# Weights laid out in DRAM as the stream of tiles, and the opening's modulation tiles as stationary operands, in an f32 transformer kernel on one Trainium2 core

## The reference

```python
shift, scale, gate = jnp.split(jax.nn.silu(c) @ w_mod + b_mod, 3, axis=-1)
shift_c, scale_c, gate_c = jnp.split(jax.nn.silu(c_ctx) @ w_mod + b_mod, 3, axis=-1)
hx = rmsnorm(x, g_pre) * (1 + scale[:, None]) + shift[:, None]
hc = rmsnorm(ctx, g_pre) * (1 + scale_c) + shift_c
q, k, v, ga, uf, gf, zc, bc, cc, gc = split_cols(hx @ w_in, PROJ_SIZES)
```

## Time and profile before

| | |
|---|---|
| Median of 3 runs | 1942.44 us (1939.84 to 1943.55) |
| The profiled execution: its time | 1941.8 us |
| Its span in the profile | 1940.0 us |
| Granted TensorE clock, mean | 0.995 |
| VectorE, ScalarE, GpSimd busy | 43%, 42%, 36% of the span |
| Read from DRAM | 178.10 MB |
| DMA packets | 199589, of which 168957 are under 2 KB |

### The profile page before, as it was taken

One profiled execution on the slowest core, in us unless ns is written; L12 is line 12 of the kernel. 1 busy time (PEld: TensorE's weight loads), 2 busy tenths in 40 slices (PEclk: granted clock), 3 DMA queues, 4 the chain that ended last, 5 costly groups with the idle time before them and its releaser, 6 DMA issues.

```text
span 1940.0 us, 26619 instructions
## 1 busy us (share of the span) xinstructions
PE 1895.1 (98%) x10294; PEld 1610.3 (83%) x10294; DVE 827.5 (43%) x1871; ACT 818.7 (42%) x1573; POOL 693.5 (36%) x542
## 2 busy tenths in 40 slices
PE   8999989999899999999999999999999999999997
PEld 4897889878689888888988888888888898888886
DVE  3657866265567264576511110037267551111003
ACT  3321268363238465685332222126477432323222
POOL 0522502125430344212455454544420344544442
PEclk9999999999999999999999999999999999999999
DMA  9536322113230224211243433223320233332321
GB/s 283 166 109 217 106 45 55 44 44 116 80 87 34 90 88 118 85 34 55 77 109 87 109 87 130 87 79 109 110 82 23 69 84 109 87 106 90 130 87 44
DMA packets 199589, 181.95 MB, mean 94 GB/s; under 512 B 34823, under 2 KB 168957, under 8 KB 199465
## 3 DMA queue, kind: packets, MB, share of 16 engines
q1 hardware_dynamic: 193432, 168.93, 29.0%
q10 hardware_dynamic: 6032, 11.33, 1.9%
HBM read 178.10 MB, written 5.41 MB: 95 GB/s over the span
## 4 chain that ended last, share of the span: by engine, by line
PE 84%; DVE 5%; ACT 3%; issue 2%; POOL 2%; DMA 2%; SPq 0%; ACTq 0%; DVEq 0%
PE ps L1368 23%; PE ps L1370 22%; PE ps L1369 22%; PE ps L1962 3%; PE ps L1459 3%; PE ps L1879 3%; POOL w_lo L760 2%; DMA raw<-in_w_in 2%; PE ps L1426 2%; PE ps L1445 2%; PE ps L1980 2%; DVE acc L2172 1%; PE ps L1489 1%; ACT w_hi L815 1%; PE ps L1389 1%
## 5 line engine op out<-in xcount | busy, mean ns | idle before, releaser
L760 POOL TENSOR_TENSOR w_lo<-raw,w_hi 128x512 fp32r<-128x512 f32 (+2 forms) x507 | 668.5, 1351 | 1147.7 <-ACT w_hi L815 1147.6
L815 ACT ACTIVATE w_hi<-raw 128x1024 fp32r<-128x1024 f32 (+3 forms) x256 | 252.4, 1032 | 300.9 <-PE ps L1370 190.9
L1368 PE MATMUL ps<-g_hi,w_lo 128*128 128x512 f32 (+1 forms) x928 | 348.4, 375 | 1.4 <-POOL w_lo L760 1.4
L1369 PE MATMUL ps<-g_lo,w_hi 128*128 128x512 f32 (+1 forms) x928 | 347.5, 374 | 0.0
L1370 PE MATMUL ps<-g_hi,w_hi 128*128 128x512 f32 (+1 forms) x928 | 347.4, 374 | 0.0
L1368 PEld LDWEIGHTS ps<-g_hi,w_lo 128*128 128x128 f32 x928 | 174.7, 188 | 33.6 <-issue 1.7
L1370 PEld LDWEIGHTS ps<-g_hi,w_hi 128*128 128x128 f32 x928 | 174.7, 188 | 31.4
L1369 PEld LDWEIGHTS ps<-g_lo,w_hi 128*128 128x128 f32 x928 | 174.7, 188 | 30.8
L1368 PE MATMUL ps<-h_hi,w_lo 128*128 128x512 f32 (+1 forms) x496 | 181.8, 367 | 8.1 <-ACT cz L972 4.5
L2715 DVE TENSOR_TENSOR tmp_f<-ps,tmp_f 128x512 f32<-128x512 f32 x44 | 30.4, 692 | 370.7 <-PE ps L1370 370.7
L1369 PE MATMUL ps<-h_lo,w_hi 128*128 128x512 f32 (+1 forms) x496 | 175.7, 354 | 0.0
(11 more groups left out here) (310 smaller groups left out, 3426.8 us busy)
## 6 DMA issues: line engine op xcount, KB each, us to landing
raw<-in_w_in SPq DMA_DIRECT2D x30, 1024.0 KB, 5.4
raw<-in_w_mod SPq DMA_DIRECT2D x24, 1024.0 KB, 6.1
raw<-in_w_gate SPq DMA_DIRECT2D x44, 512.0 KB, 4.0
raw<-in_w_up SPq DMA_DIRECT2D x44, 512.0 KB, 5.3
raw<-in_w_down SPq DMA_DIRECT2D x22, 1024.0 KB, 4.9
raw<-in_w_out SPq DMA_DIRECT2D x8, 1024.0 KB, 11.6
strips<-bias_rows ACTq DMA_DIRECT2D x18, 256.0 KB, 3.1
raw<-in_w_in SPq DMA_DIRECT2D x16, 256.0 KB, 4.6
```

What stands on the lines that cost most here:

```text
L760: pool.tensor_tensor(w_lo[:, i % SPLIT, a:e], raw_of(what)[:, a:e], w_hi[:, i % SPLIT, a:e].bitcast(F32), ALU.subtract).then_inc(s_tile_lo ...
L815: act.activation(w_hi[:, i % SPLIT, a:b], raw_of(what)[:, a:b], ACT.Copy).then_inc(s_tile_hi.sem, s_tile_hi.nth((what, n)))
L1368: pe.matmul(o, lhs[1], rhs[0], start=first, stop=False)
L1369: pe.matmul(o, lhs[0], rhs[1], start=False, stop=False)
```

## The change

1. The host lays all tiles of the stream one behind another in one array `tiles` (tile, partition, 2048 columns), so that every tile is one transfer with one run of up to 8 KB for each partition. The vectors come as one array `columns` (128 x 118), already turned, loaded by ScalarE's queue into `vec_t`.
2. The opening's modulation tiles become the stationary operand: for each tile 2 x 8 products with a 128 x 128 block of `raw` stationary and `cond` (2 columns) moving, which give columns at once. `mod_row`, `fold`, `first_row`, `first_turn` and both transposes of the vectors are gone.
3. Two of the eight tiles (j = 5 and j = 2) get homes of their own, in the second slots of `w_hi` and `w_lo`, which nothing else uses yet; they are loaded between and behind the halves of `x`. The first query tile is fetched ahead of the last two modulation tiles.
4. The orders of the opening on ScalarE, TensorE, VectorE and GpSimd are rewritten. There are 18 warming products in one piece where there were 7 and 4.

The core of the diff:

```diff
+def _stream():
+
+    s = []
+    for l in range(DEPTH):
+        tiles = _mix_tiles(l)
+        if l == 0:
+            first = [((0, "mod", j), [_rows("w_mod", 0, 0, 256 * j, KD, 256)]) for _, _, j in FIRST]
+            tiles = first[0:3] + [first[5], tiles[0]] + first[6:] + tiles[1:]
+            tiles_apart = first[3:5]
...
+def _laid_out(w):
+
+    stream, apart = _stream()
+    t = np.zeros((len(stream + apart), P, TILE), np.float32)
+    for n, (_, parts) in enumerate(stream + apart):
+        for name, l, row, col, k, c, to, pitch in parts:
+            for j in range(k):
+                t[n, :, to + pitch * j:to + pitch * j + c] = w[name][l, row + P * j:row + P * j + P, col:col + c]
+    return t
...
+        opening = [at(f"opening{i}", [P, TILE], names[where][0] + 4 * TILE) for i, where in enumerate(("w_hi", "w_lo"))]
...
-                for into, src in loads:
-                    sp.dma_start(into(raw[:, n % RAW, :]), src).then_inc(landed_sems[n % RAW], 16)
-                if n < 2:
-                    for dst, src in vectors[4 + 5 * n:9 + 5 * n]:
-                        sp.dma_start(dst, src).then_inc(s_vectors.sem, 16)
-                if n in (2, 3):
-                    t = 2 * (n - 2)
-                    sp.dma_start(res[:, t:t + 2, :], I["x"][0, t * P:(t + 2) * P, :].rearrange("(t p) d -> p t d", p=P)).then_inc(s_x_landed[n - 2].sem, 16)
-                if n == 4:
+                sp.dma_start(raw[:, n % RAW, 0:width(what)], I["tiles"][n, :, 0:width(what)]).then_inc(landed_sems[n % RAW], 16)
+                if n == 2:
+                    for i in range(2):
+                        sp.dma_start(res[:, 2 * i:2 * i + 2, :], I["x"][0, 2 * i * P:(2 * i + 2) * P, :].rearrange("(t p) d -> p t d", p=P)).then_inc(s_x_landed[i].sem, 16)
+                        sp.dma_start(opening[i][:], I["tiles"][len(stream) + i]).then_inc(s_opening[i].sem, 16)
+                if n == 3:
                     sp.dma_start(res_c[:], I["ctx"][0].rearrange("(t p) d -> p t d", p=P)).then_inc(s_x_landed[2].sem, 16)
...
-            for m in range(3):
-                for k in (2 * m, 2 * m + 1):
-                    ctx_lo(0, k)
-                if m > 0:
-                    tile_lo_part(0, 2 * m - 2)
-                    tile_lo_part(0, 2 * m - 1)
-            ctx_lo(0, 6)
-            ctx_lo(0, 7)
+            for p in range(4):
+                tile_lo_part(0, p)
+            for k in range(KD):
+                ctx_lo(0, k)
...
                         if i >= SPLIT:
                             act.wait_ge(s_mm.sem, s_mm.at(("tile", splits[i - SPLIT])))
+                        elif i == 1:
+                            act.wait_ge(s_mm.sem, s_mm.at(("tile", apart[1])))
...
+            act.dma_start(vec_t[:, 0:NV], I["columns"]).then_inc(s_vectors.sem, 16)
+            act.dma_start(ident[:], I["ident"]).then_inc(s_ident.sem, 16)
+            act.wait_ge(s_vectors.sem, 16)
             act.activation(cond[:], vec_t[:, 0:16].rearrange("p (s k) -> p k s", s=2), ACT.Silu).then_inc(s_cond.sem, s_cond.nth(0))
...
             squares(0, 2)
-            first_row(3)
             root((0, "pre", "x"), 8, XT)
+            first_rows(0)
             act.wait_ge(s_x_landed[2].sem, 16)
             squares(0, 4)
             root((0, "pre", "ctx"), 8 + XT, CT)
-            first_row(4)
-            first_rows(0)
-            first_row(5)
+            split_next()
+            first_rows(1)
             first_ctx(0, 0)
-            first_rows(1)
-            first_row(6)
-            split_next()
+            first_rows(2)
             first_ctx(0, 1)
-            first_rows(2)
-            first_row(7)
             first_ctx(0, 2)
             first_rows(3)
...
-            warm(7)
-            pe.wait_ge(s_cond_in.sem, 16 * len(cond_vectors))
-            pe.transpose(ps[:, 7, 0:16], vec[0:16, :], ident[0:16, 0:16]).then_inc(s_vec_mm.sem, s_vec_mm.nth(0))
-            emptied[7] = s_vec_t.after(0)
-            warm(4)
+            warm(18)
...
-                for k in range(KD):
-                    m = pe.matmul(o, cond[:, k, :], raw_of(what)[:, 256 * k:256 * k + 256], start=k == 0, stop=k == KD - 1)
+                for c in range(2):
+                    for k in range(KD):
+                        a = 256 * k + P * c
+                        m = pe.matmul(ps[:, ROW_BANK[i], 2 * c:2 * c + 2], raw_of(what)[:, a:a + P], cond[:, k, :], start=k == 0, stop=k == KD - 1)
...
             first_mod(0)
-            pe.wait_ge(s_vectors.sem, 16 * len(vectors))
-            pe.transpose(ps[:, 2, 0:NV], vec[0:NV, :], ident[0:NV, 0:NV]).then_inc(s_vec_mm.sem, s_vec_mm.nth(1))
-            emptied[2] = s_vec_t.after(1)
-            first_mod(1)
-            first_turn(0)
-            first_mod(2)
-            first_turn(1)
-            first_turn(2)
-            first_mod(3)
-            first_turn(3)
-            first_mod(4)
+            pe.wait_ge(s_ident.sem, 16)
+            for i in range(1, 5):
+                first_mod(i)
             turn_x(0, 0)
             turn_x(0, 1)
-            first_turn(4)
             first_mod(5)
             turn_x(0, 2)
             turn_x(0, 3)
-            turn_ctx(0, 0)
-            first_turn(5)
             first_mod(6)
             turn_x(0, 4)
             turn_x(0, 5)
+            turn_ctx(0, 0)
+            first_mod(7)
             turn_ctx(0, 1)
-            first_turn(6)
-            first_mod(7)
-            turn_ctx(0, 2)
-            first_turn(7)
             q0_rows(0, 0)
             turn_x(0, 6)
             turn_x(0, 7)
+            turn_ctx(0, 2)
             q0_rows(0, 1)
             turn_ctx(0, 3)
...
             for t in range(XT):
                 first_norm(t)
+            first_shift(0)
+            first_in(4)
             first_square(5, 2)
             first_var("ctx", XT, CT, (4,))
-            first_shift(0)
+            first_rows(0)
+            first_in(5)
+            first_shift(1)
             inverse((0, "pre", "ctx"), 8 + XT, CT)
             for t in range(XT, NT):
                 first_norm(t)
-            first_in(4)
-            first_rows(0)
-            first_shift(1)
-            first_in(5)
             first_rows(1)
```

More of the change, by code:

```diff
@@ new lines, in _width, with _rows, _square, _mix_tiles @@
+def _width(what):
+    if what[1] == "up":
+        return 2 * C_HEADS * (QC + HD)
+    if what[1] == "dft":
+        return 4 * (EVEN + ODD) + (4 * EVEN if what[0] < DEPTH - 1 else 0)
+    return {"c": 4 * 416, "av": 4 * 384}.get(what[1], TILE)
+def _rows(name, l, row, col, k, n, to=0, pitch=None):
+    return name, l, row, col, k, n, to, pitch or n
+def _square(name, l, ch, kh):
+    return _rows(name, l, 512 * kh, 512 * ch, 4, 512)
+def _mix_tiles(l):
+    t = []
+    for j in range(2):
+        heads = (2 * j, 2 * j + 4, 2 * j + 1, 2 * j + 5)
+        t.append(((l, "q", j), [_rows("w_in", l, 0, HD * h, KD, HD, HD * i, 256) for i, h in enumerate(heads)]))
+    for what, a in (("kv", 512), ("uf", 1280), ("gf", 1536), ("zc", 1792), ("bc", 2048), ("cc", 2304), ("gc", 2560)):
+        t.append(((l, what), [_rows("w_in", l, 0, a, KD, 256)]))
+    for j in range(2):
+        t.append(((l, "ga", j), [_rows("w_in", l, 0, 768 + 256 * j, KD, 256)]))
+    t.append(((l, "dft"), [_rows("dft", 0, 0, 0, 1, _width((l, "dft")))]))
+    return t
@@ new lines, in _stream @@
+def _stream():
[6 more added lines that the diff above has]
+            tiles_apart = first[3:5]
+        for tile in tiles:
+            s += [(WEIGHED[m], [_square("w_mod", WEIGHED[m][0], *WEIGHED[m][2:])]) for m in GOES_BEFORE.get(tile[0], ())]
+            s.append(tile)
+        s += [((l, "out", ch, kh), [_square("w_out", l, ch, kh)]) for ch, kh in ((0, 1), (0, 0), (1, 0), (1, 1))]
+    for l in range(DEPTH):
+        s += _second_tiles(l)
+    return s, tiles_apart
@@ new lines, in _laid_out, with _columns @@
+def _laid_out(w):
[5 more added lines that the diff above has]
+                t[n, :, to + pitch * j:to + pitch * j + c] = w[name][l, row + P * j:row + P * j + P, col:col + c]
+    return t
+def _columns(w):
+    rows = [w["c"], w["c_ctx"]]
+    for l in range(DEPTH):
+        rows += [w[n][l] for n in ("b_mod", "g_pre", "g_post", "conv_w", "conv_b")]
+    rows += [w["q_norm_g_2"], w["kv_norm_g_2"]]
+    return np.ascontiguousarray(np.concatenate([np.asarray(r, np.float32).reshape(-1, P) for r in rows]).T)
@@ L237, in _program @@
         acc = [[at("acc00", [P, 512], acc_at), at("acc01", [P, 512], acc_at + 2048)],
[L238 to L239 removed]
+               [at("acc10", [P, 512], acc_at + 4096), acc11]]
+        assert 6144 <= 2 * 4 * TOK
         tmp_m = at("tmp_m", [P, 2, 512], names["q1"][0])
@@ L343, in _program @@
         s_mod_c = Signal(nc, ctx, seen, "mod_c")
-        s_mod_row = Signal(nc, ctx, seen, "mod_row")
+        s_opening = [Signal(nc, ctx, seen, f"opening{i}") for i in range(2)]
         s_mod_x = Signal(nc, ctx, seen, "mod_x")
@@ L490, in _program @@
+        stream, apart = _stream()
```

(18 more changed lines are left out.)

175 lines of the change are left out of this document (39 added, 136 removed).

## The result

The changed kernel takes 1966.87 us (median; 1964.93 to 1967.98), the kernel before on the same chip 1942.35: ratio 1.0126, 95% interval 1.0114 to 1.0138. It is 24.5 us slower. The forecast was 1930.5, and the time lies above the range too.

The account below looks back on a forecast made before the run. TensorE, busy 1895.1 of 1940.0 us, was taken as the bound, with transfers close in the opening; 9.7 (opening) + 1.5 (transfers) + 0.7 (clock) = 11.9 us off, giving 1930.5 us; own range 1927 to 1938, overall 1926 to 1960.

Parts of the forecast that it names:

- everything sought in the opening: Opening: first query product starts at 40.7 us instead of 50.38, 9.7 us earlier, bounds 4.4 to 11.4.
- a thin record at 0.11 us: Opening's modulation tiles: 32 records with two columns moving each, taken at 3.55 us a tile, range 3.4 to 4.2.
- The rival: Opening: two-column products drop the clock to 1.2 GHz, 7.1 us a tile, 14.5 us slower, 1957 us; chance 0.35.
- 2.61 us a megabyte: Weight tile transfers: 8 KB rows taken at 401 GB/s, 2.61 us a tile instead of 2.98 at 352.
- the better bound of the estimate: Tile transfers: 8 KB rows somewhat better than 4 KB rows, 2.5 us a tile, an estimate.
- 1.5 from legs: Body: four `w_in` transfers on the chain shorten by 0.37 us each, 1.5 us in sum, bounds 0 and 2.0.
- 0.7 from the clock behind the wait: At 165.73 us: with the wait cut to 3.7 us the slow clock may stay away, 0 to 1.4 us.
- first thin product: Opening: the first modulation product starts at 7.1 us, where it was 8.8.
- The "no wait" at `turn_x(0)`: Opening, behind tiles 0 to 4: norms of `x` ready at 25.0 us, TensorE through its tiles at 24.9.
- The third rival: Opening: new order starves the query rows, their start slips to 48 us or more, 1939 to 1942 us; chance 0.05.

Follow-up runs that it names:

- after: The profiled trace of the changed kernel, all parts of the change against the kernel before; the kernel took 1966.87 us, ratio 1.0126.
- eight fillers: Changed kernel at the old buffer addresses, with eight unread ones-by-ones products of 128 columns put between the two-column products of each modulation tile: 1978.22 us, ratio 1.0194.
- the run with the old places: Changed kernel with 448 unused bytes ahead of `mod`, so every buffer from there on lies where the kernel before had it: 1953.48 us, ratio 1.0066.
- the run with thin products alone: Kernel before with only its modulation products turned, tiles stationary and two `cond` columns moving; loads, order and buffer addresses left: 1962.64 us, ratio 1.0112.
- wide products: Changed kernel at the old buffer addresses with `cond` stationary again and 256 columns moving, row copies and turns back: 1940.21 us, ratio 0.9995.
- the mended order: 256-column version of the changed kernel at old addresses, with `x` and `ctx` norms and the root moved ahead of later modulation sums and rows: 1932.31 us, ratio 0.9955.

## Why the prediction was wrong, point by point

**What bounds the kernel.** Right: TensorE's queue in the opening, TensorE all over. It was also read that only about 45 us could come from waits. What followed was not drawn: where TensorE is 98% busy, a change of 1 to 3% in the pitch of its long products (12.3 us here) is worth as much as everything sought in the opening (9.7).

**The step that failed first: the clock.** The sum took a thin record at 0.11 us, from the earlier trace rows, stretches of about 1 us between wide products. They show the price of such a record at 2.4 GHz, which held (0.107), and nothing of the clock under 18 us of them in a row. In the changed kernel the clock fell to 0.50 at 13 us and a record took 0.207 us: 6.62 us a tile in place of 3.55, and the opening became 13.1 us longer in place of 9.7 shorter. The rival had the mechanism, the place and nearly the size: the first query product at 64 to 67 us, measured 63.49; 6.62 us a tile for 7.1; 14.5 us slower, measured 11.8 with the places put back. Its 1957 is nearer to 1966.87 than the forecast, but by this term alone; it had the places no more than the forecast did. It got a chance of 0.35 because "TensorE has instructions in flight all the time". The runs show that this does not keep the clock up: busy 4.00 of 4.00, clock 0.50, in after and with eight fillers. What the trace of before held for it was the stretch at 0.55 to 0.60, which ended under wide products only. The decision between 0.35 and, say, 0.7 was not to be had from the rows, but a run of operations more than ten times as long as any in the trace should not have been priced as the likeliest case. In the run with the old places the last thin tile even ran at full clock and the next query products at half; why, no run shows:

```profile
56.06 3.93 PE L1466 MATMUL ps<-cond,raw 128*128 128x2 f32 x32
```

The Trainium skill, "TensorE: Matmul & The Clock Gate", section Part 4: PE-mode transpose, says only that transposes are not counted as work in the same way; that was named in the rival, and the trace agrees in so far as the turns between thin tiles brought nothing back. The same page of the Trainium skill, section Seeing it yourself, warns that recorded clock events are unreliable; the run with thin products alone bears the caution out, with 1.00 in the row beside transposes at 1.95 us for eight.

**The step that was not there: the places.** The diff shows `vec` going and `eps_c` and `centre` coming; the prediction costed what these buffers do and put at nothing, without a reason, where the others go. That term measured 12.3 us, half of the loss. The trace of before has no row that would have given a price. The Trainium skill, "SBUF — State Buffer", section Who interferes with whom, gives TensorE independent read ports for the moving operand and for the weight load, and says that it never waits on anyone. Here its two reads, or something that goes by their addresses, do hamper each other by 2 to 8 ns in 227; the measurement decides. By that rule the experiments with places would all have given 1932.

**The layout.** 2.61 us a megabyte was taken; 415 to 426 GB/s make it 2.46 to 2.53, at the better bound of the estimate. The share of a core near 358 GB/s that the Trainium skill, "DMA: Bandwidth & Descriptors", section Where 436 GB/s comes from, takes to bind loads from HBM, weighed in the prediction, does not bind this stream, on one core alone: the measurement decides. The gain: 1.5 from legs and 0.7 from the clock behind the wait, 2.2 together, were expected; 2.5 (span) and 3.7 (medians) came. That the sum is near is in part luck. At 165 the legs gave 1.1 where 0.74 was priced, and the clock took it back where it was to give 0.7; the slow stretch that shortened is the one behind 504.63.

**The opening.** Columns and `cond` as expected (silu done at 6.4 us), first thin product at 7.56 (7.1), loads in time; `split_next` ahead of the rows starved nothing. The "no wait" at `turn_x(0)`, 25.0 against 24.9, hung on an unqueued VectorE: the norms stood behind `first_in(3)`. With wide products this was 1.5 us of wait and the fall of the clock behind it. The third rival (starving, 0.05) gave 1939 to 1942, and this run has 1940.21; but it named the split and the context parts, and what came late was `xn`, behind a sum on VectorE. That the opening can be 5.7 us shorter, kept to the end, is shown by the mended order; that it could be 9.7 with thin products was only so at a clock that they did not get. The mended kernel's 1932.31 lies close to the forecast of 1930.5, but by other terms: 5.4 from the opening, the rest from waits and from the clock behind them.

**The sum as it came**, in the profiled executions: opening with its clock +14.8 (the distance at 83 us), places +13.5 (the distance at 1920 us in the kernel before with the new places), layout -2.4: 25.9, against 25.5 at 1920 us in after. By the medians it is 12.3 and 11.8, 24.1 against 24.5.

## What to carry to other kernels

Before turning a product round so that few columns move, ask what TensorE's clock does meanwhile, and price the turned form at 1.2 GHz unless a trace shows a long run of it at 2.4; the wide form cost about the same per tile here at 2.4 GHz (3.55 us for 3.4) and the clock stayed up under it. When a change adds or removes a buffer, work out where every operand behind it lands: keep the distance from stationary to moving operands what it was (here a multiple of 512 bytes), and if the time moves, count products in a window where nothing waits, before and after. And an order that hides a wait on paper must be read in the queue of the engine that produces, not only of the one that waits.

## What the runs showed of the hardware

- TensorE's granted clock fell from 1.00 to 0.50 with records in flight in all 4.00 us of every window, when they moved two columns each (0.207 us a record for 0.107). With eight products of 128 columns more in each tile it fell too; with sixteen it stayed at 1.00, in one execution.
- A row of 1.00 from the start of a trace can mean that no change was recorded: products of 0.63 us for 0.40 gave it away. In that trace the first record of the clock stands at 73.5 us.
- An f32r product of 512 columns follows the last in 226.7 to 234.3 ns at the same clock, by the distance from its stationary to its moving operand modulo 512 bytes (0 is best of the nine measured), whether other engines run or not: up to 32 us of 1932.
- One core drew 415 to 426 GB/s from DRAM with runs of 8 KB per partition, where runs of 1 KB gave 351 to 373.
